# A two-layer encoder with routed experts: the second block's coefficient matrix in four sets of two tokens, half its weights on GpSimd, and gathered rows of V added in PSUM

## What is computed

```python
# experts: 8 heads x 16 of 16384 experts for each token, gb: their gates
u = u_tab[eb]                                   # rows of 2048 channels
h = jnp.einsum("thkd,td->thk", u, xb)
coef = gb * jax.nn.gelu(h, approximate=False)
return jnp.einsum("thk,thkd->td", coef, v_tab[eb])
```

## Time and profile before

| what | value |
|---|---|
| median of 3 runs | 3661.9 us (3659.53 to 3665.86) |
| the profiled execution's own time | 3661.7 us |
| its span, first to last instruction | 3659.9 us |
| PE (TensorE matmul) busy | 2957.0 us, 81% |
| DVE (VectorE) busy | 2573.8 us, 70% |
| ACT (ScalarE) busy | 847.4 us, 23% |
| POOL (GpSimd) busy | 2063.9 us, 56% |
| HBM traffic over the span | 302 GB/s |

### The profile page before, as it was taken

One profiled execution on the slowest core, in us unless ns is written; L12 is line 12 of the kernel. 1 busy time (PEld: TensorE's weight loads), 2 busy tenths in 40 slices (PEclk: granted clock), 3 DMA queues, 4 the chain that ended last, 5 costly groups with the idle time before them and its releaser, 6 DMA issues. The chain is left out here.

```text
span 3659.9 us, 46828 instructions
## 1 busy us (share of the span) xinstructions
PE 2957.0 (81%) x15193; PEld 2284.4 (62%) x15193; DVE 2573.8 (70%) x3476; ACT 847.4 (23%) x1343; POOL 2063.9 (56%) x1470
## 2 busy tenths in 40 slices
PE   8968895776777689999499998957677776899993
PEld 7854694666767654444297986956667766544441
DVE  4997679787888666666744455797878886666667
ACT  1002431222333530000133443311123335300000
POOL 6794175777777346677400001657767773477774
PEclk9987997888899789999799999978888997899997
DMA  7421447999999569999755434469999995699998
GB/s 245 138 91 46 161 138 288 422 422 422 421 422 422 192 247 405 402 409 409 302 184 184 139 124 164 138 268 422 422 422 421 422 422 212 228 403 402 409 404 304
DMA packets 293734, 1106.84 MB, mean 302 GB/s; under 512 B 21957, under 2 KB 120837, under 8 KB 220677
## 3 DMA queue, kind: packets, MB, share of 16 engines
q0 software_dynamic: 147456, 805.37, 54.5%
q1 hardware_dynamic: 146182, 300.22, 22.8%
HBM read 1103.41 MB, written 2.10 MB: 302 GB/s over the span
## 5 line engine op out<-in xcount | busy, mean ns | idle before, releaser
L525 POOL DMA_INDIRECT ring<-in_peer_u,index_now x512 | 848.2, 1657 | 367.8 <-issue 115.1
L1364 DVE SCALAR_TENSOR_TENSOR ring<-ring,x_tok 128x2048 f32<-128x2048 f32 x384 | 879.2, 2298 | 227.3 <-DMA ring<-in_peer_u,index_now 220.2
L791 PE MATMUL ps<-all_v,mix 128*128 128x512 f32 x1984 | 851.8, 592 | 0.0
L791 PEld LDWEIGHTS ps<-all_v,mix 128*128 128x128 f32 x1984 | 377.0, 190 | 474.5 <-issue 474.5
L548 POOL DMA_INDIRECT work<-in_peer_v,index_add x344 | 450.1, 1309 | 330.2 <-DVE x_tok L1407 148.9
L762 PE MATMUL ps<-x_dot,work 128*128 128x128 f32 x4096 | 539.5, 295 | 99.0 <-ACT work L1007 67.6
L1407 DVE SCALAR_TENSOR_TENSOR x_tok<-work,coef,x_tok 128x1024 f32<-128x1024 f32 x344 | 441.3, 1285 | 242.1 <-DMA work<-in_peer_v,index_add 241.4
L762 PEld LDWEIGHTS ps<-x_dot,work 128*128 128x128 f32 x4096 | 522.3, 210 | 120.6 <-ACT work L1007 81.6
L756 PE MATMUL ps<-ident,ring 128*128 128x128 f32 x2048 | 344.7, 339 | 306.4 <-DMA ring<-in_peer_u,index_now 299.7
L489 POOL TENSOR_TENSOR w_lo<-ring,w_hi 128x2048 fp32r<-128x2048 f32 x34 | 159.3, 4688 | 665.6 <-ACT w_hi L890 665.6
L756 PEld LDWEIGHTS ps<-ident,ring 128*128 128x128 f32 x2048 | 306.5, 177 | 328.7 <-DMA ring<-in_peer_u,index_now 197.2
(11 more groups left out here) (181 smaller groups left out, 3713.7 us busy)
## 6 DMA issues: line engine op xcount, KB each, us to landing
all_v<-in_peer_v SPq DMA_DIRECT2D x248, 512.0 KB, 6.7
ring<-in_conv_w_in SPq DMA_DIRECT2D x16, 2048.0 KB, 9.1
ring<-in_peer_w_q SPq DMA_DIRECT2D x16, 2048.0 KB, 8.5
ring<-in_attn_w_kv SPq DMA_DIRECT2D x16, 2048.0 KB, 8.6
ring<-in_conv_w_out SPq DMA_DIRECT2D x8, 2048.0 KB, 7.9
ring<-in_attn_w_q SPq DMA_DIRECT2D x8, 2048.0 KB, 8.5
ring<-in_attn_w_o SPq DMA_DIRECT2D x8, 2048.0 KB, 7.9
ring<-in_peer_u,index_now POOLq DMA_INDIRECT x512, 14.4
```

Of the source, the lines that this page charges most:

```text
L525: pool.indirect_dma_start(u_tile(s), None, u_tab, bass.IndirectOffsetOnAxis(ap=index_now[:, half, s:s + 1], axis=0)).then_inc(u_row[s], 16)
L791: mm = pe.matmul(ps[:, dense_bank(tb, q), :], mix[tb][:, row, :], tile[:, q * 512 - HALF:(q + 1) * 512 - HALF], start=False, stop=True, sk ...
L1364: dve.scalar_tensor_tensor(out=u_tile(s), in0=u_tile(s), scalar=1.0, in1=x_tok[:, tb, :], op0=ALU.mult, op1=ALU.mult, accum_out=coef[:, tb ...
```

## The change

- The expert sum's left half is accumulated in PSUM: `add` reads and writes banks 0 and 1 (block A) and 4 and 5 (block B) in place of `x_tok`. Alpha times the left half of x comes into these banks by a product of TensorE with `alpha_ident`, after `turn_slots(1)` and ahead of the rounds; VectorE waits for it (`x_scaled`) before its first mask of block B. The two scalings L1443 go. The dense sums move to banks 2 and 3, 6 and 7.
- Block B's masks are made for two tokens at a time, both in one instruction of 512 elements (`mask_set`), in four sets of buffers. Sets 0 and 1 are weighed on ScalarE, two instructions each (`weigh_set`); sets 2 and 3 on Pool, one instruction of 256 elements each. A round is four sets. A bank of four products (2 or 3) holds two sets. ScalarE's order in a round: weigh set 0, copy bank 1 of the round before, weigh set 1, copy bank 0 of this round.
- The alpha products of the right half come after the last copy of `mix` (they use the same banks), ahead of the dense product.
- VectorE does one add at the end of each of the first 10 rounds (16 rounds before). Pool issues the first 24 gathers one by one from `index_v` without a copy of the indices: six ahead of block B's rounds, one at the end of each of the first ten rounds, eight behind the last round.

```diff
-FIRST_ADDS = 16
+SETS = 4
+PAIR = 2
+FIRST_ADDS = 10
+OPEN_GATHERS = 24
...
+        hot_set = nc.alloc_sbuf_tensor_at("hot_set", [P, SETS, 2, PAIR, P], F32, offset=x_chan_at)
...
         def dense_bank(tb, q):
 
-            return Q + (Q // 2) * tb + q - Q // 2
+            return Q * tb + q
...
+        def slot_bank(tb):
+
+            return (Q + 2) * tb
+
+        def mix_bank(tb, b):
+
+            return 2 * tb + b
+
+        def add_sum(tb):
+
+            return ps[:, Q * tb:Q * tb + Q // 2, :].rearrange("p a b -> p (a b)")
...
+                for n in range(G_RING):
+                    if n == 2:
+                        pool.wait_ge(h_steps, 2 + 2 * NT * GROUPS * TB * (layer + 1))
+                    gather_add(n)
+                pool.wait_ge(slot_taken, layer * TB + 2)
+                for r in range(ROUNDS):
+                    for m in range(SETS // 2, SETS):
+                        n = r * SETS + m
+                        pool.wait_ge(set_made, layer * ROUNDS * SETS + n + 1)
+                        pool.tensor_tensor(out=hot_set[:, m, 0, :, :], in0=hot_set[:, m, 0, :, :],
+                                           in1=by_slot[:, 1, 2, n * PAIR:(n + 1) * PAIR].unsqueeze(2).to_broadcast([P, PAIR, P]),
+                                           op=ALU.mult).then_inc(set_weighed_pool, 1)
+                    if r < FIRST_ADDS:
+                        gather_add(G_RING + r)
+                for n in range(G_RING + FIRST_ADDS, OPEN_GATHERS):
+                    gather_add(n)
...
                 turn_slots(1)
-                with pe.Fori(0, BATCHES // 2) as i:
-                    mix_pair(1, i)
-
+                for tb in range(TB):
+                    for q in range(Q // 2):
+                        mm = residual(tb, q)
+                    mm.then_inc(x_scaled, 1)
+                with pe.Fori(0, ROUNDS) as i:
+                    mix_round(i)
+
+                pe.wait_ge(mix_taken, 2 + BATCHES * TB * (layer + 1))
                 for tb in range(TB):
                     for q in range(Q // 2, Q):
-                        pe.matmul(ps[:, dense_bank(tb, q), :], alpha_ident[:, :], x_tok[:, tb, q * 512:(q + 1) * 512],
-                                  start=True, stop=True, skip_group_check=True)
+                        residual(tb, q)
...
+                def mix_round(i):
+
+                    for m in range(SETS):
+                        at = layer * ROUNDS * SETS // 2 + m % 2 + 1
+                        pe.wait_ge(set_weighed if m < SETS // 2 else set_weighed_pool, i * (SETS // 2) + at)
+                        if m % 2 == 0:
+                            pe.wait_ge(mix_taken, i * 2 + ((layer * TB + 1) * BATCHES + m // 2 + 1))
+                        for k in range(PAIR):
+                            at = (m % 2 * PAIR + k) * P
+                            mm = pe.matmul(ps[:, mix_bank(1, m // 2), at:at + P], hot_set[:, m, 1, k, :], hot_set[:, m, 0, k, :], start=True, stop=True)
+                        mm.then_inc(set_used, 1)
...
+                def weigh_round(i, first):
+
+                    weigh_set(i, 0)
+                    if not first:
+                        take_mix(1, i - 1, 1)
+                    weigh_set(i, 1)
+                    take_mix(1, i, 0)
...
-                    dve.scalar_tensor_tensor(out=x_tok[:, tb, 0:HALF], in0=add_tile(k), scalar=coef[:, tb, slot], in1=x_tok[:, tb, 0:HALF],
+                    dve.scalar_tensor_tensor(out=add_sum(tb), in0=add_tile(k), scalar=coef[:, tb, slot], in1=add_sum(tb),
                                              op0=ALU.mult, op1=ALU.add).then_inc(g_used, 1)
...
+                def mask_set(r, m):
+
+                    n = layer * ROUNDS * SETS + r * SETS + m
+                    t = (r * SETS + m) * PAIR
+                    dve.wait_ge(set_used, n + 1)
+                    by_m = by_slot[:, 1, 0:2, t:t + PAIR].unsqueeze(3).to_broadcast([P, 2, PAIR, P])
+                    dve.tensor_tensor(out=hot_set[:, m, :, :, :], in0=iota_f[:, :].unsqueeze(1).unsqueeze(1).to_broadcast([P, 2, PAIR, P]),
+                                      in1=by_m, op=ALU.is_equal).then_inc(set_made, 1)
...
-                for tb in range(TB):
-                    dve.tensor_scalar(x_tok[:, tb, 0:HALF], x_tok[:, tb, 0:HALF], ALPHA, None, ALU.mult).then_inc(x_scaled, 1)
 
                 uses = [-(-(TILES - k) // G_RING) for k in range(G_RING)]
                 dve.wait_ge(slot_taken, layer * TB + 2)
                 dve.wait_ge(x_scaled, (layer + 1) * TB)
-                for b in range(BATCHES):
-                    masks(1, b)
-                    if b % 2:
-                        n = b // 2
+                dve.wait_ge(mix_ready, (layer + 1) * BATCHES)
+                for n in range(ROUNDS):
+                    for m in range(SETS):
+                        mask_set(n, m)
+                    if n < FIRST_ADDS:
                         add(n % G_RING, n % TB, ((layer * uses[n % G_RING] + n // G_RING + 1) * 16, G_RING + layer * TILES + n - 1),
                             slice(n // TB, n // TB + 1))
```

More of the change, by code:

```diff
@@ L68, in build @@
     BATCHES = P // BATCH
+    ROUNDS = P // (SETS * PAIR)
     ALPHA = (2.0 * LAYERS) ** 0.25
@@ L505, in _ @@
                         base = (layer * TB + tb) * GROUPS + part * groups
-                        copied = layer * (TB * GROUPS + SLOTS // 3 + 1) + tb * GROUPS + part * groups
+                        copied = layer * (TB * GROUPS + SLOTS // 3 + 1 - OPEN_GATHERS // G_RING) + tb * GROUPS + part * groups
                         def gather(first, last, opening):
@@ L550, in gather_adds @@
                             bass.IndirectOffsetOnAxis(ap=index_add[:, half, k % TB, k // TB:k // TB + 1], axis=0)).then_inc(g_row[k], 16)
-                with pool.Fori(0, SLOTS // (2 * per)) as i:
+                with pool.Fori(opened // 2, SLOTS // (2 * per)) as i:
                     for half in range(2):
@@ L564, in _ @@
             pe.sem_inc(h_steps, 2)
+            pe.sem_inc(set_used, SETS)
             def turn_x(n):
@@ L795, in peer @@
                 full = NKEY // D_RING - 1
-                pe.wait_ge(mix_taken, 2 + BATCHES * TB * (layer + 1))
                 for i in range(full):
@@ L1023, in peer @@
                 take_turned(1, 1)
-                made = layer * TB * 2 * BATCHES
+                made = layer * 2 * BATCHES
                 def weigh_pair(i):
@@ L1029, in weigh_pair @@
                         act.wait_ge(hot_made, i * 4 + (made + 2 * b + 2))
-                        weigh_hot(0, i, b)
+                        weigh_hot(i, b)
                         if b:
@@ L1042, in peer, with weigh_set @@
                 act.wait_ge(slot_taken, layer * TB + 2)
-                made = (layer * TB + 1) * 2 * BATCHES
-                with act.Fori(0, BATCHES // 2) as i:
-                    for b in range(2):
-                        act.wait_ge(hot_made, i * 4 + (made + 2 * b + 2))
-                        weigh_hot(1, i, b)
-                        if b:
-                            take_mix(1, i, 0)
+                def weigh_set(i, m):
+                    act.wait_ge(set_made, i * SETS + (layer * ROUNDS * SETS + m + 1))
+                    for k in range(PAIR):
+                        last = act.activation(hot_set[:, m, 0, k, :], hot_set[:, m, 0, k, :], ACT.Copy,
+                                              scale=by_slot[:, 1, 2, bass.ds(i * (SETS * PAIR) + (m * PAIR + k), 1)])
+                    last.then_inc(set_weighed, 1)
+                def weigh_round(i, first):
[4 more added lines that the diff above has]
+                    take_mix(1, i, 0)
+                with act.Fori(0, 1) as i:
+                    weigh_round(i, True)
+                with act.Fori(1, ROUNDS) as i:
+                    weigh_round(i, False)
+                with act.Fori(ROUNDS - 1, ROUNDS) as i:
                     take_mix(1, i, 1)
@@ L1435, in peer @@
                 for b in range(BATCHES):
-                    masks(0, b)
+                    masks(b)
                     if b < 28 and b % 2:
```

69 lines of the change are left out of this document (33 added, 36 removed).

## The result

The changed kernel takes 3611.93 us (median of 4 runs, 3610.41 to 3612.89) beside 3663.15 us for the kernel before on the same chip; the ratio is 0.9865, with a 95% interval of 0.9852 to 0.9878. The prediction was 3650 with a range from 3634 to 3678: the direction was right, the forecast gain was less than a quarter of the measured one, 11.7 us for 51.2 by the medians (49.8 between the two profiled executions). The profiled execution took 3611.92 us, its span 3610.0.

The account below looks back on a forecast made before the run. It took the end to be set by how early full DMA use begins and how many gathers are done by then. Gains of 13.0 - 8.4 = 4.6 and 15.5 - 8.4 = 7.1, together 11.7 us, took 3661.7 to 3650, range 3634 to 3678.

Parts of the forecast that it names:

- start of the rounds: Block B: VectorE's first mask waits for alpha products, so TensorE begins the rounds 4.8 and 2.3 us later.
- rounds up to VectorE's release: Block B, each layer: rounds gain 18.8 us, less 1.0 lost because VectorE's release comes closer to the last product's end.
- from the release to the last add: Gathers after block B's rounds: six more to move while DMA is full, 8.4 us given back in each layer.
- The length of a round: Block B: 4.15 us for all 16 rounds, 66.4 us for 85.2, a gain of 18.8 a layer.
- Without: masks and Pool one after the other 2.5 + 1.44 and handovers, 4.1, or 4.25: Block B's rounds without an add: masks and Pool's products exclude each other, 4.1 us, or 4.25 at low clock.
- The other chain, through ScalarE's order: Block B's round: bank 1 copy, set 1 weighing, three sets of products; 4.25 us at lower clock, 2.9 at higher.
- the rival with 17%: Faster rounds: TensorE stays at 2.4 GHz and Pool's work hides; 3627 us, half of it 3638; chance 0.17.
- Pool's issues become shorter ... DMA is full there, so they give nothing: Dense stage: Pool's issues shorten without two SBUF inputs beside them, but gain nothing because DMA is full.
- Six fewer adds: Block B's rounds, ten adds for 16: gathers moved later at 1.4 us each, 8.4 us given back a layer.
- The adds in PSUM: VectorE's adds of 1024 elements: 1.28 us each, bounded by 1.2 and 1.6.
- The dense stage: Dense product sets its own length, 449 us, with DMA full; it starts some 13 us earlier.
- The slower rival: Block B's rounds: Pool and VectorE exclude each other in series; 3679 us, 3683 at the bound; chance 0.25.

Follow-up runs that it names:

- e7: Changed kernel with 16 adds in the rounds, VectorE's alpha wait moved to the first add, block B's right alpha products earlier: 3602.87 us, ratio 0.9839.
- e2: Changed kernel with all four sets weighed on ScalarE and none on Pool: 3646.36 us, ratio 0.9955.
- e3: Kernel before the change, with only the left half's sums moved to PSUM: 3645.15 us, ratio 0.9963.
- e12: Changed kernel with an in-place product of 256 elements on Pool added ahead of each looped gather: 3679.71 us.
- e4: Changed kernel with 16 adds and gathers in the rounds in place of 10: 3604.81 us, ratio 0.9847.
- e1: Changed kernel with the left half's adds back in SBUF (x_tok), scaled by VectorE: 3632.91 us, ratio 0.9917.

## Why the prediction was wrong

Measured from the traces in the prediction's own terms, both layers together (the start of the rounds is counted from the start of the last dot product with U to their first product):

| term | forecast | measured |
|---|---|---|
| start of the rounds later | +7.1 | +1.4 |
| rounds up to VectorE's release | -35.6 | -49.5 |
| from the release to the last add | +16.8 | +1.0 |
| outside the expert sum | 0 | -2.9 |
| sum | -11.7 | -50.0 |

- **The start of the rounds.** From the last dot product with U to the first product of the rounds it was 23.2 and 22.4 us, and is 24.6 and 22.5 (24.6 and 23.9 in the second profile). The alpha products took 3.60 us in both layers, for 6.9 and 4.4: TensorE was at its higher clock. That clock differs between executions (e7's took 4.91). The mechanism was right, the size was off by the clock.
- **The length of a round** is the first step that failed, and most of it in the rounds without an add. "I take 4.15 for all 16" came to 66.4 us; the 16 rounds took 59.6 us in the first layer, from 1240.56 to 1300.15, a gain of 25.6 for 18.8. Between the adds the forecast's 4.1 was met on average (4.06 and 3.86), but not as it was made up: the bare sum of VectorE's work, 3.74, was nearly the usual round (3.60), and the long ones came, all but one, with an issue of Pool held beside the masks, which the sum did not count. From the tenth add to the eleventh, six rounds of masks alone, it took 20.2 and 21.9 us, 3.2 and 3.4 a round once the add's 1.2 is taken off. The forecast had "Without: masks and Pool one after the other 2.5 + 1.44 and handovers, 4.1, or 4.25". Masks and Pool do hold each other up, but two Pool products added some 0.7 us to four masks of 2.5 (3.24), and not 1.44 and handovers. The other chain, through ScalarE's order, was worked out for TensorE at the lower clock (its own terms, 1.5 and 2.85, give 4.35 and not 4.25); the granted clock was 0.88 in the rounds, and at the higher clock the same chain has 2.9 and is not the bound. The prediction had this as the rival with 17%. What made the clock rise no run shows; it rose in every run with Pool's half (median record 275 ns) and not in e2 or e3 (421).
- **"Pool's issues become shorter ... DMA is full there, so they give nothing"** is the second step that failed. They did become shorter, 0.94 us, and the adds in PSUM gave 5.7 and 10.7 us (e3). The share of 1.02 had been read as a ceiling. The earlier trace rows show Pool busy for 296 of the 420 us; what they don't show, and the trace of before had, is how little of the rest was a wait for adds: 34 us of 420 in the second layer (the line under e12). That this is the reason is argued, as said there.
- **Six fewer adds**, 1.4 us each, was nearly right in size (1.1 by e4). It was hidden in the result by the step before.
- **The adds in PSUM** took 1.290 us in the middle for the 1.28 taken: right.
- **The dense stage** kept its 449 us: right. It starts 24.1 us earlier, for the 13 forecast.
- **The slower rival**, Pool and VectorE in series, had a mechanism that exists: its "issue of the gather is held by the masks too; TensorE and with it the reuse of sets 2 and 3 come late" is what the long intervals show, and with the adds in SBUF every round is 4.38 us (e1). Its price was not reached. In strict turn, four masks (2.5) and two Pool products at their shortest (0.61 each) would be 3.7 us without an add; 3.24 was measured.
- **Outside the expert sum**, 2.9 us: the stretch from the last add of the first layer to the last dot product of the second is 1241.0 before, 1237.6 after, and 1240.9 in the second profile of the same changed kernel. So it lies within the spread between executions, and no effect is shown.

## What to carry to other kernels

A full DMA share does not say that the queue which gets the remainder is at its limit: look at how long the engine that issues it still waits for anything. When VectorE shares a stage with work or DMA issues on Pool, try one of its two inputs in PSUM where the sum can live there: it was worth 15 us of 3660 by itself here (e3), and some 20 beside Pool's products (e1). Moving the weights to Pool paid even with the adds in SBUF (rounds of 68.6 us for 89.8). When some rounds of a loop hold less work than the others, price them by themselves. When several waits in a chain through TensorE are shortened, work out the chain at both clocks, since the same change may move the kernel from one to the other.

## What was not expected of the hardware

- A VectorE add of 1024 elements from SBUF and PSUM into PSUM takes 1.290 us in the middle, 1.285 with all in SBUF; beside a Pool product the second took up to 1.632 us and the first never more than 1.292.
- Pool's issue of an indirect DMA that started beside masks, which have two SBUF inputs, took 2.98 us in three cases of ten and 1.17 to 1.25 us in the others.
- Pool's issue of an indirect DMA is 0.94 us beside adds in PSUM and 1.42 us beside adds in SBUF, in stages that are otherwise the same.
- An in-place product of 256 elements on Pool took 0.88 us for the 0.55 of another place in the program, and a memset with a wait on its own semaphore 0.85 us in all, of which 0.33 was the memset.
